# A hybrid decoder trunk on one core: another order of norms and weight splits, and upper weight parts read first

## The reference

```python
def layer_norm(x, g, b):
    mu = jnp.mean(xf, axis=-1, keepdims=True)
    var = jnp.mean(jnp.square(xf - mu), axis=-1, keepdims=True)
    y = (xf - mu) * lax.rsqrt(var + NORM_EPS) * g + b
...
    z = x @ w_in                                  # the mixer: 1024 x 2048
    xr, g = z[..., :LRU_WIDTH], z[..., LRU_WIDTH:]
    xc, new_buf = causal_conv(xr, conv_buf, conv_w, conv_b)
    hs, hT = rglru(xc, h0, w_a, b_a, w_i, b_i, lam)
    y = (hs * gelu(g)) @ w_o
...
    z = x @ w_gu                                  # the MLP: 1024 x 5632, then 2816 x 1024
    return (silu(z[..., :D_FF]) * z[..., D_FF:]) @ w_down
...
        xp = layer_norm(ALPHA * xp + mp, ln_g[i, 0], ln_b[i, 0])
        xp = layer_norm(ALPHA * xp + swiglu(...), ln_g[i, 1], ln_b[i, 1])
```

## Time and profile before

| what | us |
|---|---|
| median of three runs | 1454.02 |
| lowest, highest | 1452.93, 1455.72 |
| the profiled execution | 1453.68 |
| its span in the profile | 1451.8 |
| TensorE busy (share of the span) | 1407.5 (97%) |
| DVE, ACT, POOL busy | 654.3, 526.9, 214.3 |
| DMA queue of the weights, share of 16 engines | 25.8% |
| mean granted TensorE clock | 0.995 |

### The profile page before, as it was taken

The page is one execution under the profiler, slowest core; times in us unless marked ns, Lnnn a source line. Parts: engine busy times, 40 slices in busy tenths (PEclk is TensorE's granted clock), DMA queues, the critical chain, the costliest instruction groups (busy, mean ns, idle before and its releaser), DMA issues.

```text
span 1451.8 us, 26919 instructions
## 1 busy us (share of the span) xinstructions
PE 1407.5 (97%) x10447; PEld 1296.6 (89%) x10447; DVE 654.3 (45%) x971; ACT 526.9 (36%) x856; POOL 214.3 (15%) x318
## 2 busy tenths in 40 slices
PE   9989999899999999999999989999999999999997
PEld 9846666556989999999999979999899999999996
DVE  4546666633473323222333567886723332322335
ACT  4236555522343222122222458864422221222234
POOL 0020000000344000000001412346510000000033
PEclk9999999999999999999999989999999999999999
DMA  8231011032223332223332213222332322223301
GB/s 213 63 89 27 21 25 23 24 94 88 88 59 88 87 109 81 84 60 87 87 120 73 61 42 96 61 87 59 88 91 87 120 70 61 84 87 98 120 1 63
DMA packets 180837, 111.15 MB, mean 77 GB/s; under 512 B 25896, under 2 KB 179069, under 8 KB 180768
## 3 DMA queue, kind: packets, MB, share of 16 engines
q1 hardware_dynamic: 180176, 109.41, 25.8%
q0 software_dynamic: 592, 0.79, 0.2%
HBM read 107.15 MB, written 3.02 MB: 76 GB/s over the span
## 4 chain that ended last, share of the span: by engine, by line
PE 86%; DVE 7%; ACT 3%; issue 1%; POOL 1%; SPq 0%; DMA 0%; DVEq 0%; ACTq 0%; POOLq 0%
PE ps L517 54%; PE ps L546 6%; PE ps L768 3%; PE ps L606 3%; PE ps L782 3%; DVE wl L1499 2%; PE ps L802 2%; PE ps L1099 1%; PE ps L785 1%; PE ps L946 1%; PE ps L663 1%; DVE xc L1900 1%; PE ps L759 1%; ACT wh L1164 1%; PE ps L901 1%
## 5 line engine op out<-in xcount | busy, mean ns | idle before, releaser
L517 PE MATMUL ps<-xh,wh 128*128 128x280 f32 x1568 | 330.2, 292 | 5.3 <-DVE wl L1499 4.7
L517 PE MATMUL ps<-xh,wl 128*128 128x280 f32 x1568 | 331.2, 292 | 0.0
L517 PE MATMUL ps<-xl,wh 128*128 128x280 f32 x1568 | 328.7, 291 | 0.0
L517 PEld LDWEIGHTS ps<-xh,wh 128*128 128x128 f32 x1568 | 249.4, 188 | 7.2 <-issue 4.5
L517 PEld LDWEIGHTS ps<-xh,wl 128*128 128x128 f32 x1568 | 250.5, 189 | 0.0
L517 PEld LDWEIGHTS ps<-xl,wh 128*128 128x128 f32 x1568 | 248.0, 188 | 0.0
L1164 ACT ACTIVATE wh<-raw 128x2048 fp32r<-128x2048 f32 (+2 forms) x79 | 162.9, 2062 | 203.1 <-PE ps L517 179.3
L1499 DVE TENSOR_TENSOR wl<-raw,wh 128x2048 fp32r<-128x2048 f32 (+2 forms) x79 | 197.6, 2502 | 85.4 <-ACT wh L1164 85.4
L1834 DVE TENSOR_TENSOR ht<-sg,ps 128x560 f32<-128x560 f32 x44 | 32.5, 738 | 269.0 <-PE ps L517 264.8
L1411 ACT ACTIVATE hh<-ht 128x560 f32 (+1 forms) x44 | 29.6, 672 | 262.1 <-DVE ht L1834 262.1
L2024 POOL TENSOR_TENSOR acc<-xT 128x560 f32<-128x560 f32 x4 | 5.6, 1398 | 753.5 <-DVE xT L1725 648.5
(11 more groups left out here) (337 smaller groups left out, 2443.5 us busy)
## 6 DMA issues: line engine op xcount, KB each, us to landing
raw<-in_ffn_w_gu SPq DMA_DIRECT2D x176, 256.0 KB, 3.6
raw<-in_ffn_w_down SPq DMA_DIRECT2D x48, 384.0 KB, 4.3
raw<-in_lru_w_in SPq DMA_DIRECT2D x16, 512.0 KB, 4.6
Ctok<-in_cache_latent SPq DMA_DIRECT2D x48, 128.0 KB, 2.1
raw<-in_mla_w_o SPq DMA_DIRECT2D x16, 256.0 KB, 3.7
raw<-in_ffn_w_down SPq DMA_DIRECT2D x16, 256.0 KB, 5.1
raw<-in_lru_w_o SPq DMA_DIRECT2D x16, 256.0 KB, 3.4
wq<-in_mla_w_q_up SPq DMA_DIRECT2D x16, 144.0 KB, 2.4
```

Of the source, the lines that this page charges most:

```text
L517: mm = pe.matmul(ps[:, 1024 * jp + 512 * h:1024 * jp + 512 * h + TH], w[:, k, col:col + P], x[:, k, h * TH:(h + 1) * TH], start=(k == 0 an ...
```

## The change

It changes five things.

1. DVE's `moments` subtracts both centres before the variance. In norms 0 and 2 residual(4, 1) stands behind the variance and ahead of the reciprocal, residual(5, 1) behind the second scaling. In norms 1 and 3 (`late`) residual(4, 1) stands behind the second scaling and residual(5, 1) behind the sixth. ACT's squares follow in the same places.
2. The split of the first opening chunk stays behind tile 3 of DVE (1 of ACT) in norms 0 and 2 and moves behind tile 5 (3 of ACT) in norm 1. The split of the second opening chunk moves behind the squares of tiles 6 and 7 on ACT and behind rest(1) on DVE.
3. TensorE's first opening pass waits for the upper parts of its chunk and runs three k with them alone ahead of the lower ones; the second pass runs all eight k so. The moments of half 1 move to the start of the second pass (0 and 2), or into the first (k = 3 and 5, norm 1).
4. `lru_input` runs all matmuls on the upper parts (32), then those on the lower (16), and waits for each where it needs it.
5. In norm 2 the early sum has three tiles; POOL makes one addition less, the mean uses the weight 1/384, and `moment_sum` adds tile 3 by one fp32 matmul more in each half.

```diff
+EARLY = (4, 4, 3, 4)
+SUMS = (0, 5, 10, 14)
...
             def moment_sum(n, h):
-                pe.wait_ge(n_acc, 5 * n + 4 + h)
+                pe.wait_ge(n_acc, SUMS[n] + EARLY[n] + h)
                 pe.wait_ge(n_accB, 2 * n + h + 1)
                 pe.matmul(bk(1 + 4 * h), ones[:, 0, :], acc[:, toks(h)], start=True, stop=False)
+                for k in range(EARLY[n], 4):
+                    pe.wait_ge(n_shp, 2 * n + 2)
+                    pe.matmul(bk(1 + 4 * h), ones[:, 0, :], xT[:, k, toks(h)], start=False, stop=False)
...
+                    for k in range(ahead):
+                        ready(k)
+                        for s in tiles_of:
+                            for i in range(2):
+                                step(k, s, i)
+                    pe.wait_ge(lo_ok, c + t // 2 + 1)
+                    for k in range(ahead):
+                        for s in tiles_of:
+                            step(k, s, 2)
+                    for k in range(ahead, KD):
+                        ready(k)
+                        for s in tiles_of:
+                            for i in range(3):
+                                mm = step(k, s, i)
...
-                pe.wait_ge(lo_ok, c + 1)
-                two(0, 0, ready(0))
-                pe.wait_ge(lo_ok, c + 2)
-                pe.wait_ge(f0_ok, c)
-                two(2, 0, moments)
+                pe.wait_ge(hi_ok, c + 1)
+                two(0, 0, first, 3)
+                pe.wait_ge(hi_ok, c + 2)
+                pe.wait_ge(f0_ok, c)
+                two(2, 0, moments(0) if tiles == 4 else lambda k: None, KD)
                 two(0, 1, ready(1))
...
             def lru_input(c, u):
+                pe.wait_ge(hi_ok, c + 1)
+                pe.wait_ge(f0_ok, c)
+                for k in range(KD):
+                    for x in (xh, xl):
+                        for h in range(2):
+                            pe.matmul(ps[:, 512 * h:512 * h + TH], hi[:, k, 0:P], x[:, k, toks(h)],
+                                      start=(k == 0 and x is xh), stop=False)
                 pe.wait_ge(lo_ok, c + 1)
-                pe.wait_ge(f0_ok, c)
-                dense(0, u, KD, 256, 0, xh, xl, t0_ok)
+                for k in range(KD):
+                    for h in range(2):
+                        mm = pe.matmul(ps[:, 512 * h:512 * h + TH], lo[:, k, 0:P], xh[:, k, toks(h)],
+                                       start=False, stop=(k == KD - 1))
+                mm.then_inc(t0_ok, 1)
...
+                late = n % 2
                 moments(0)
-                square(4, 1)
                 root(0)
-                square(5, 1)
+                if not late:
+                    square(4, 1)
                 for k in range(KD):
                     out(k, 0)
-                    if k == 1 and n < 3:
+                    if k == 1:
+                        square(4 if late else 5, 1)
+                    if k == (3 if late else 1) and n < 3:
                         split_next(c + 3, 0, 0, 0)
-                    if k == 5 and n < 3:
-                        split_next(c + 4, 0, 0, 0)
+                    if k == 4 and late:
+                        square(5, 1)
                 square(6, 1)
                 square(7, 1)
+                if n < 3:
+                    split_next(c + 4, 0, 0, 0)
                 moments(1)
...
-                    centre(0, h)
+                    for k in range(2):
+                        centre(k, h)
                     dve.wait_ge(n_var, 2 * n + h + 1)
...
-                    centre(1, h)
+                    if h == 0 and not late:
+                        residual(4, 1)
                     dve.wait_ge(n_root, 2 * n + h + 1)
...
                 rest(0)
-                residual(4, 1)
                 moments(0)
-                residual(5, 1)
                 for k in range(KD + 1):
                     if k < KD:
                         scaled(k, 0)
+                    if k == 1:
+                        residual(4 if late else 5, 1)
                     if k >= 1 and n < 3:
                         low(k - 1, 0)
-                    if k == 3 and n < 3:
+                    if k == (5 if late else 3) and n < 3:
                         split_next(c + 1, 0, 0)
-                if n < 3:
-                    split_next(c + 2, 0, 0)
+                    if k == 5 and late:
+                        residual(5, 1)
                 residual(6, 1)
                 residual(7, 1)
                 rest(1)
+                if n < 3:
+                    split_next(c + 2, 0, 0)
                 moments(1)
```

More of the change, by code:

```diff
@@ L48 @@
 LRU_C = 8.0
-EARLY = 4
+EARLY = (4, 4, 3, 4)
+SUMS = (0, 5, 10, 14)
 NEG = -1.0e30
@@ L596, in opening, with two, step @@
             def opening(c, n, done1, tiles=4):
-                def two(t, h, ready):
+                def two(t, h, ready, ahead=0):
                     u = (c + t // 2) % 2
                     hi, lo = (w[u][:, 0:W_D].rearrange("p (k n) -> p k n", k=KD) for w in (wh, wl))
-                    for k in range(KD):
-                        ready(k)
-                        for s in range(min(2, tiles - t)):
-                            for i, (w, x) in enumerate(((hi, xh), (hi, xl), (lo, xh))):
-                                mm = pe.matmul(bk(2 * (t + s) + h), w[:, k, P * s:P * s + P], x[:, k, toks(h)],
-                                               start=(k == 0 and i == 0), stop=(k == KD - 1 and i == 2))
+                    tiles_of = range(min(2, tiles - t))
+                    def step(k, s, i):
+                        w, x = ((hi, xh), (hi, xl), (lo, xh))[i]
+                        return pe.matmul(bk(2 * (t + s) + h), w[:, k, P * s:P * s + P], x[:, k, toks(h)],
+                                         start=(k == 0 and i == 0), stop=(k == KD - 1 and i == 2))
+                    for k in range(ahead):
+                        ready(k)
+                        for s in tiles_of:
[10 more added lines that the diff above has]
+                                mm = step(k, s, i)
                             if h == 1 and k == KD - 1:
@@ L615, in ready, with moments, there, first @@
                     return at
-                def moments(k):
-                    if k == (1 if tiles > 3 else 3):
-                        moment_sum(n, 1)
-                    if k == (3 if tiles > 3 else 6):
-                        moment_square(n, 1)
-                pe.wait_ge(lo_ok, c + 1)
-                two(0, 0, ready(0))
-                pe.wait_ge(lo_ok, c + 2)
+                def moments(at):
+                    def there(k):
+                        if k == at:
+                            moment_sum(n, 1)
+                        if k == at + 2:
+                            moment_square(n, 1)
+                    return there
+                def first(k):
+                    ready(0)(k)
+                    if tiles == 3:
+                        moments(3)(k)
+                pe.wait_ge(hi_ok, c + 1)
+                two(0, 0, first, 3)
+                pe.wait_ge(hi_ok, c + 2)
                 pe.wait_ge(f0_ok, c)
-                two(2, 0, moments)
+                two(2, 0, moments(0) if tiles == 4 else lambda k: None, KD)
                 two(0, 1, ready(1))
@@ L1051, in lru_input @@
             def lru_input(c, u):
-                pe.wait_ge(lo_ok, c + 1)
-                pe.wait_ge(f0_ok, c)
-                dense(0, u, KD, 256, 0, xh, xl, t0_ok)
+                hi, lo = (w[u][:, 0:W_D].rearrange("p (k n) -> p k n", k=KD) for w in (wh, wl))
+                pe.wait_ge(hi_ok, c + 1)
[5 more added lines that the diff above has]
+                                      start=(k == 0 and x is xh), stop=False)
+                pe.wait_ge(lo_ok, c + 1)
+                for k in range(KD):
[3 more added lines that the diff above has]
+                mm.then_inc(t0_ok, 1)
             def lru_branch(c, u):
@@ L1506, in split_next @@
                     split(c + 1, 1 - u, w)
-            for n, v in enumerate((1.0 / D, 1.0 / QL_R, 1.0 / KV_R, 1.0 / (EARLY * P))):
+            for n, v in enumerate((1.0 / D, 1.0 / QL_R, 1.0 / KV_R, 1.0 / (4 * P))):
                 dve.memset(ones[:, n, :], v).then_inc(s_ones, 1)
@@ L2015, in total @@
             def total(base, n):
-                for k in range(1, EARLY):
+                for k in range(1, EARLY[n]):
                     c = base + k // 2
@@ L2022, in total @@
                     if k > 1:
-                        pool.wait_ge(n_acc, 5 * n + k - 1)
+                        pool.wait_ge(n_acc, SUMS[n] + k - 1)
                     pool.tensor_tensor(acc[:], xT[:, 0, :] if k == 1 else acc[:], xT[:, k, :], ALU.add).then_inc(n_acc, 1)
@@ L2026, in total @@
                 for k in range(2, 4):
+                    if k >= EARLY[n]:
+                        pool.wait_ge(f1_ok, base + k // 2 + 1)
                     pool.tensor_tensor(xT[:, k, :], xT[:, k, :], mid[:], ALU.subtract).then_inc(n_shp, 1)
```

5 lines of the change are left out of this document (2 added, 3 removed).

## The result

The changed kernel takes 1435.88 us (median of 4 runs, 1435.41 to 1435.95) against 1454.26 (4 runs) of the kernel before beside it: a ratio of 0.9874 [0.9861, 0.9886] (the brackets are a 95% interval), 1.3% less. A second set of 5 runs beside another 9 of the kernel before gave 1435.81 and 0.9876 [0.9860, 0.9891]. The forecast was 1434.4. The profiled execution took 1435.41, its span is 18.2 us shorter than in the kernel before.

A forecast was written before the change was run, and what follows sets the result against it. TensorE, busy 1407.5 of 1451.8 us, was taken as the bound, so only its waits and low clock could be won. 2.9 + 3.9 + 6.0 + 7.1 - 0.4 = 19.5 us off 1453.68 gave 1434.2, median 1434.4; range 1431.5 to 1440.6.

The forecast's parts named there:

- Norm 0: First norm: TensorE's first and third waits go, about 1.2 us for ACT's split stays; 2.9 us gained.
- Norm 1: Second norm: the 1.00 us wait ends, 0.5 us of the 3.84 stays, full clock returns; 6.0 us gained.
- Norm 2: Third norm: 2.9 us as in the first, plus 1.95 for POOL's sum, less 0.95 for tile 3; net 3.9 us.
- Norm 3: Last norm: DVE's second centre ahead of the variance delays root, reciprocal and transposes by 0.36 us; loss 0.4 us.
- The mixer: RG-LRU mixer, chunks 39 to 44: waits for lower weights end, 13.87 us per chunk; 7.1 us gained after deductions.
- the 0.3 that I took off for gates that wait once: Mixer: estimated 0.3 us deducted because gates wait once for DVE after TensorE's jump ahead at chunk 39.
- 0.4 for a tail of DVE that reaches the output chunks 0.2 us late, twice: Mixer's output chunks: DVE finishing 0.2 us late, twice, deducts 0.4 us from the mixer's gain.
- rival B: DVE or ACT holds the mixer's cycle at 14.4 or 14.8 us: 2.6 or 4.6 us return, 1437.0 to 1439.0; chance 0.15.
- A: Waits left in norms 0, 1 and 2 lower TensorE's clock: 1437.4 to 1440.6 us; chance 0.15.
- C: Mixer: DVE's convolutions meet POOL's work and stretch; at 18.5 us per chunk the kernel takes 1457.4 us; chance 0.02.
- D: Waits only move: ACT, behind two squares per norm, gives back DVE's gain and the mixer waits for gates: 1453; chance 0.03.
- signs of being right: Profile after: named waits gone or about 0.5 to 1 us, mixer chunks 13.9 us apart, no 0.50 clock, last reciprocal 0.4 later.

## Why the prediction was right, and the step that was not

**Norm 0.** Forecast 2.9, measured 3.37 (m0 to m1). DVE's reciprocal was forecast at 404.95 and came at 405.16. TensorE's first wait went, and the wait for ACT's split stayed, as said: from 420.02, where the next matmul could have started, to 420.97, so 0.95 and not 1.2. Half 1 was forecast to start at 429.3; the first low part ends at 428.19 + 0.51 = 428.70 and TensorE starts at 429.10, with m0 0.26 later. So 3.02 us had been won there (431.86 less 428.84) where 2.6 was forecast, and the pace gave 0.35 where I had 0.3. From the sum at 420.97 to 429.10 are 8.13 us, so the fp32 pairs cost 1.97 and not 2.14.

DVE in norm 0, half 1, of the changed kernel, against 428.25 and 431.30 of the earlier trace rows:

```profile
425.14 1.91 DVE L1823 RECIPROCAL ps<-stat 128x280 f32<-128x280 f32 x1 [0.50 <-ACT stat L1401]
...
428.19 0.51 DVE L1838 SCALAR_TENSOR_TENSOR xl<-xT,vec,xh 128x280 fp32r<-128x280 f32 x1 [0.18 <-ACT xh L1406]
```

**Norm 1.** Forecast 6.0, measured 5.96 (m1 to g0). The program is 3.11 us earlier there (3.37 - 0.26); with that added back, DVE's split of chunk 38 ends at 838.1 (forecast 837.9), its reciprocal starts at 839.6 (839.5), the half's first low part ends at 843.2 (843.0), and the wait for it prints 0.60 (0.5). The clock stays up behind it. The sum at tile 3, said to wait for nothing, waited 0.21.

```profile
832.39 2.56 DVE L1541 TENSOR_TENSOR wl<-raw,wh 128x2304 fp32r<-128x2304 f32 x1 [1.96 <-ACT wh L1201]
...
836.52 1.91 DVE L1823 RECIPROCAL ps<-stat 128x280 f32<-128x280 f32 x1 [0.50 <-ACT stat L1401]
...
839.57 0.51 DVE L1838 SCALAR_TENSOR_TENSOR xl<-xT,vec,xh 128x280 fp32r<-128x280 f32 x1 [0.18 <-ACT xh L1406]
```

**Norm 2.** Forecast 3.9, of which 1.95 for POOL's sum and 0.95 back for tile 3. POOL's sum: g7 to m2 is 27.54 to 27.55 in the variants with the split or the tail moved, where the clock stayed up behind yo, against 29.58, so 2.04. m2 to m3 gained 2.51 where 2.9 - 0.95 = 1.95 stood, again 0.5 above. Putting the fourth tile back cost 0.90, or 1.07 with the clock alike.

**Norm 3.** Forecast -0.4, measured -0.29 and 0.27 back when undone.

**The mixer: here the step failed.** Forecast 7.1, measured 4.87: 5.07 (g0 to yo), less the 0.93 behind yo, of which all but 0.2 comes back before m2 (2.77 - 2.04 = 0.73). The first part of that term was right: no wait for lower weights, full clock. Chunks 39 to 44 start at 858.16 and 928.38, 70.22 us where five times 13.87 is 69.35: 0.87 lost, against the 0.3 that I took off for gates that wait once. 0.65 of it is the one cycle of 14.52 in which those gates wait (0.34 printed); the other 0.22 is TensorE's own pace: with yl first the gates' inputs are ready 1.5 us early and the chunks still start 13.92 apart, not 13.87. Then the term that was mis-sized: **"0.4 for a tail of DVE that reaches the output chunks 0.2 us late, twice"**. From chunk 44's start to yo are 15.88 us, and 14.05 in the kernel before: 1.83, and 0.2 more for the clock. 0.57 + 1.43 + 0.2 make the 2.2. It stood on the sentence that with 12.19 and 12.31 us of work in 14.81 "neither holds 13.87". Busy time bounds an engine that works by itself. DVE and ACT hand work to each other twice in a cycle, and the way round, 13.93 us, is what bounds both, though from 896.67 to 910.60 DVE is busy for 12.19 and ACT for 12.08 of the 13.93 us. That is rival B's mechanism, with a cycle as long as TensorE's 13.92, so that it shows as one late arrival and not as five long cycles.

**The rivals.** A, a lower clock behind the waits that stay: at 0.60, 0.79 and 0.80 it stayed up, in every profiled execution (granted clock 1.00 over the 4.5 us behind each). The Trainium skill ("TensorE: Matmul & The Clock Gate", Part 1) was weighed there with its free-running activity window; for those waits no run here shows it, for the 1.80 us one see below. B was right in kind, 2 us and not 2.6 to 4.6. C did not come: no input chunk took over 14.6, though POOL's 0.65 us sit in the loop. D came in one place: of the 6.9 us won in the input chunks 1.83 moved to the first output chunk. Of the signs of being right one failed, "no 0.50 clock between 400 and 1440 us": behind yo seven matmul pairs stood 0.47 us apart. And one input chunk of the five, at 14.52 us, lies over the 14.3 that was to show the forecast wrong; the others took 13.88 to 13.97.

**The sum.** 3.37 + 5.96 + 4.87 + (2.04 + 2.51) - 0.29 = 18.46 where 19.5 stood: norms 0 and 2 gave 1.1 more, the mixer 2.2 less. With m0 0.26 later and a median 0.5 above the profiled execution (0.34 before), and since 1434.2 + 0.34 is 1434.5 and not 1434.4, that is the 1.5 us between 1434.4 and 1435.88. The terms were off by up to 2.2 us; that the total came nearer is in part luck, as they were off both ways.

## What to carry to other kernels

Before calling two engines free because each is busy less than a cycle, follow the cycle round through both, hand-overs and table loads included: if the way round is as long as the cycle of the engine that bounds, a delay never heals, and what stands outside that loop (here moving the split behind one small subtraction) is what pays. A producer's order and its consumer's order are one change: either alone lost 1 to 2 us at the norms here where both won nearly 13. And when a wait falls, look for the next instruction that the late engine feeds: reading the upper parts first won 6.9 us in the input chunks, of which 1.8 came back one stage on, and at the first output chunk it only moved the wait on, twice.

## What the runs showed that was not expected

**The same wait, with and without a lower clock.** Behind the 1.80 us wait at yo seven of the changed kernel's matmul pairs stood 0.47 us apart, in both of its profiled executions, and in the one with norm 1 in the other order; in the kernels without the norms' new order or opening, with the split moved, the tail moved, or the fourth early tile, the same wait (1.52 to 1.80) left them 0.26 apart. Timelines of TensorE, the changed kernel and then the one with the tail moved, whose program is the same up to there:

```profile
944.95 0.67 PE L1136 MATMUL ps<-yh,wl 128*128 128x280 f32 x2
945.42 0.67 PE L1136 MATMUL ps<-yh,wh 128*128 128x280 f32 x2
```

```profile
948.51 0.42 PE L1136 MATMUL ps<-yh,wl 128*128 128x280 f32 x2
948.77 0.42 PE L1136 MATMUL ps<-yh,wh 128*128 128x280 f32 x2
```

Nor did the slow pairs begin at one distance behind the wait: 0.7 us behind its end in the first execution of the changed kernel, 1.1 in the second, 1.7 with norm 1 in the other order. The kernel without the opening has two waits of one length for the same split, 2.93 us in norm 0 and 2.94 in norm 2. Windows behind them, in the order of the earlier trace rows:

```profile
423.08:428.00 4.92, 4.92 (x31) 4.55 (x32) 1.23 (x3) 0.70 (x2) 2.42 (x4) 1.00 0.71 200
1018.97:1024.00 5.03, 5.03 (x21) 4.34 (x22) 0.10 (x1) 0.70 (x2) 0.41 (x1) 0.66 0.68 196
```

The first left the clock up, the second did not. In all profiled executions, between m0 and m3, waits of up to 1.27 us cost no clock by themselves, those of 3.84 and 5.75 always did, and those between went either way (2.51 us before the gates left it up, 1.85 and 2.16 did not). The Trainium skill ("TensorE: Matmul & The Clock Gate", Part 1) says that the clock gate's activity window is free-running. These rows agree; that the window decided here is not shown otherwise.

At yo it cost almost nothing: yo to g7 is 4.71 against 3.80, but the gates behind wait 0.44 and the last chunks 0.56 us for DVE where the clock stays up, and yo to m2 is 31.52 against 31.34.

**POOL beside DVE's split.** A copy of 24 columns by GpSimd takes 0.20 us in the kernel before and 2.54 in the changed one, where the new rhythm puts it beside DVE's split (900.16 to 902.70): it ends 0.06 us behind the split. With yl ahead of the split it is the next copy that meets it (split 927.58 to 930.13). Timelines of POOL, the kernel before, the changed one, and the one with yl first:

```profile
925.42 0.20 POOL L2076 COPY hist<-U 128x24 f32 x1
925.56 0.20 POOL L2070 COPY U<-stT 128x24 f32 x1
```

```profile
900.22 2.54 POOL L2124 COPY hist<-U 128x24 f32 x1
902.71 0.72 POOL L2118 COPY U<-stT 128x24 f32 x1
```

```profile
926.99 0.73 POOL L2124 COPY hist<-U 128x24 f32<-128x24 f32 x1
927.66 2.54 POOL L2118 COPY U<-stT 128x24 f32<-128x24 f32 x1
```

The small operation waits for the large one, whose own time does not change (2.54 us, and 2.55 before). The Trainium skill ("SBUF — State Buffer", Who interferes with whom) says that DVE and GpSimd take the port pair they share as an exclusive lock; the rows agree. It goes the other way too: beside POOL's bias add it is DVE's convolution that is 0.6 us longer (above). No engine's rows name these copies as what they waited for; with them 3 us longer POOL is busy for 8.3 us of the 13.93 us cycle.
